# A two-layer decoder trunk on one core: order of VectorE's work around low halves, and where the modulation tiles stand

## The reference, cut to what matters

```python
cond = silu(c)
for layer in range(2):
    mod = cond @ ada_w[layer] + ada_b[layer]            # 2048 x 12288, one row of cond
    sh1, sc1, g1, sh2, sc2, g2 = split(mod, 6)
    h = rms_norm(x) * (1 + sc1) + sh1
    y = even_mixer(h, ...) if layer == 0 else odd_mixer(h, ...)
    x = x + g1 * y
    h = rms_norm(x) * (1 + sc2) + sh2
    gate, up = split(h @ ffn_w_in[layer], 2)            # 2048 x 11264
    x = x + g2 * ((silu(gate) * up) @ ffn_w_out[layer])
return rms_norm(x, final_norm)

# even_mixer: one projection 2048 x 6144; 8 heads "A" (causal attention over the 256 tokens)
# and 4 heads "B", each with two softmax maps and a 256-wide value:
w = p[map 0] - lam * p[map 1]                            # the "map combination"
yb = rms_norm(w @ v, subln_w) * (1 - lambda_init)        # the "output scaling" of B
# odd_mixer: 32 query heads of 64 on 4 key/value heads, window 128, a sink logit per head
```

## Time and profile before

| | us |
|---|---|
| median of 3 runs (2286.57 to 2287.35) | 2286.96 |
| the profiled execution | 2287.97 |
| its span in the trace | 2286.2 |
| TensorE busy | 2168.9 |
| VectorE busy | 1622.3 |
| ScalarE busy | 967.0 |

### The profile page before, as it was taken

One profiled execution on the slowest core, in us unless ns is written; L12 is line 12 of the kernel. 1 busy time (PEld: TensorE's weight loads), 2 busy tenths in 40 slices (PEclk: granted clock), 3 DMA queues, 4 the chain that ended last, 5 costly groups with the idle time before them and its releaser, 6 DMA issues.

```text
span 2286.2 us, 26487 instructions
## 1 busy us (share of the span) xinstructions
PE 2168.9 (95%) x10092; PEld 1802.7 (79%) x10092; DVE 1622.3 (71%) x1683; ACT 967.0 (42%) x1261; POOL 9.9 (0%) x22
## 2 busy tenths in 40 slices
PE   3789999989999999999998999989999999999997
PEld 2668878778888888888886888878888888888885
DVE  5989888887679988777678665577665554555454
ACT  4344444444443444434444444454443344434443
POOL 0000000000000000000000000000000000000000
PEclk9899999999999999999999999999999999999998
DMA  9968878667768999977675733347765555555533
GB/s 391 421 277 314 338 300 332 269 262 295 284 270 353 386 379 378 374 295 289 264 279 203 267 125 112 121 169 286 287 254 185 200 185 185 193 192 191 196 147 147
DMA packets 82448, 594.10 MB, mean 260 GB/s; under 512 B 9296, under 2 KB 9328, under 8 KB 10672
## 3 DMA queue, kind: packets, MB, share of 16 engines
q1 hardware_dynamic: 81072, 588.29, 66.9%
q0 software_dynamic: 1280, 4.51, 0.7%
HBM read 590.66 MB, written 2.10 MB: 259 GB/s over the span
## 4 chain that ended last, share of the span: by engine, by line
PE 48%; issue 36%; DVE 9%; ACT 3%; DMA 3%; DVEq 1%; SPq 0%; POOL 0%; ACTq 0%; POOLq 0%
PE ps L1240 15%; PE ps L1242 15%; PE ps L1241 15%; DVE w_lo L748 3%; DMA gate<-in_ada 2%; PE ps L1228 2%; DVE ada_raw L752 2%; ACT w_hi L452 1%; ACT gate L522 1%; ACT ada_raw L522 1%; DVE gate L752 0%; PE ps L1302 0%; PE ps L1297 0%; PE ps L1300 0%; DMA raw<-in_ab_in 0%
## 5 line engine op out<-in xcount | busy, mean ns | idle before, releaser
L748 DVE TENSOR_TENSOR w_lo<-raw,w_hi 128x1024 fp32r<-128x1024 f32 x728 | 881.2, 1223 | 508.5 <-ACT w_hi L452 503.4
L452 ACT ACTIVATE w_hi<-raw 128x1024 fp32r<-128x1024 f32 x728 | 763.5, 1060 | 1004.5 <-PE ps L1242 825.4
L1240 PE MATMUL ps<-w_hi,xT_hi 128*128 128x512 f32 x1952 | 775.8, 397 | 36.9 <-DVE xT_lo L952 26.5
L1242 PE MATMUL ps<-w_hi,xT_lo 128*128 128x512 f32 x1952 | 766.4, 393 | 0.0
L1241 PE MATMUL ps<-w_lo,xT_hi 128*128 128x512 f32 x1952 | 766.0, 392 | 0.0
L1240 PEld LDWEIGHTS ps<-w_hi,xT_hi 128*128 128x128 f32 x1952 | 369.9, 189 | 116.2 <-DVE xT_lo L952 28.8
L1242 PEld LDWEIGHTS ps<-w_hi,xT_lo 128*128 128x128 f32 x1952 | 370.3, 190 | 79.2
L1241 PEld LDWEIGHTS ps<-w_lo,xT_hi 128*128 128x128 f32 x1952 | 371.0, 190 | 75.0
L752 DVE SCALAR_TENSOR_TENSOR ada_raw<-ada_raw,cond 128x2048 f32<-128x2048 f32 x176 | 401.7, 2283 | 17.5 <-DMA ada_raw<-in_ada 16.5
L1240 PE MATMUL ps<-w_hi,hT_hi 128*128 128x512 f32 x960 | 376.3, 392 | 0.0
L1242 PE MATMUL ps<-w_hi,hT_lo 128*128 128x512 f32 x960 | 373.9, 389 | 0.0
(11 more groups left out here) (163 smaller groups left out, 834.6 us busy)
## 6 DMA issues: line engine op xcount, KB each, us to landing
ada_raw<-in_ada SPq DMA_DIRECT2D x176, 1024.0 KB, 6.4
raw<-in_ffn_in SPq DMA_DIRECT2D x176, 1024.0 KB, 4.8
raw<-in_ffn_out SPq DMA_DIRECT2D x88, 1024.0 KB, 4.9
raw<-in_ab_in SPq DMA_DIRECT2D x48, 1024.0 KB, 8.8
raw<-in_swa_in SPq DMA_DIRECT2D x20, 1024.0 KB, 6.1
raw<-in_ab_out SPq DMA_DIRECT2D x16, 1024.0 KB, 8.4
raw<-in_swa_out SPq DMA_DIRECT2D x16, 1024.0 KB, 4.8
spare<-in_ada SPq DMA_DIRECT2D x8, 1024.0 KB, 8.3
```

Of the source, the lines that this page charges most:

```text
L452: nc.scalar.activation(w_hi[:, p % PAIRS, :, :], raw[:, t % RAW, 2 * (p % 2):2 * (p % 2) + 2, :], ACT.Copy).then_inc(hi_ready, 1)
L748: tt(w_lo[:, p % PAIRS, :, :], raw[:, (p // 2) % RAW, 2 * (p % 2):2 * (p % 2) + 2, :], w_hi[:, p % PAIRS, :, :].bitcast(F32), ALU.subtract ...
L1240: mm(out, hi[:, kt, tok], w_hi[:, q % PAIRS, k, :], start=(kt == 2 * ps0), stop=False)
L1242: last = mm(out, lo[:, kt, tok], w_hi[:, q % PAIRS, k, :], start=False, stop=(kt == 2 * ps1 - 1))
```

## The change

Five edits, all in the order of work. No arithmetic is added or removed.

1. The tile count of a phase is now in units of 2 tiles instead of 4, and a phase can have a `lag`: no tiles behind its first `lag` pairs. `AB_IN` is split into `AB1` (one unit, 10 tiles, lag 4) and `AB23` (two units, 12 tiles each); `AB_OUT` has 14 tiles (12 before) with lag 7. In the first feed-forward the three runs have, per iteration, 6, 8, 4 tiles in the inner part (4, 8, 4 before) and 8, 4, 2 in the outer (8, 4, 4 before). `C_KV` has none (4 before). The second feed-forward is as it was.
2. In the key/value block the low halves 4 to 7 stand ahead of the clearing of `work`.
3. For B units the map combination stands ahead of the fifth low half, and in `ab` the tile of pair 5 stands ahead of it.
4. For B units in `ab` the output scaling stands ahead of the tile of pair 11.
5. In the odd layer the output scaling stands one pair earlier (9 instead of 10 in `C_DVE`) and is no longer a special case at the evacuations.

```diff
-    def __init__(self, prev, n, blocks, pairs, ada, src=None, src0=0, evacs=None):
+    def __init__(self, prev, n, blocks, pairs, ada, src=None, src0=0, evacs=None, lag=0):
...
     def ada_steps(self, p):
-        n = 4 * self.ada
-        return range(n * p // (2 * self.quads), n * (p + 1) // (2 * self.quads))
+        n = 2 * self.ada
+        if p < self.lag:
+            return range(0)
+        p, of = p - self.lag, 2 * self.quads - self.lag
+        return range(n * p // of, n * (p + 1) // of)
...
-TAIL_DVE = {3: "v", 4: "tops", 5: "recip", 8: "copy1", 10: "y", 13: "lo"}
+TAIL_DVE = {4: "tops", 8: "copy1", 13: "lo"}
...
-C_DVE = {4: "tops", 6: "recip", 7: "copy1", 8: "copy3", 10: "y", 11: "lo"}
+C_DVE = {4: "tops", 6: "recip", 7: "copy1", 8: "copy3", 9: "y", 11: "lo"}
...
-    AB_IN = phase(3, 3, 8, 3, src="ab_in", src0=12, evacs=2)
-    AB_OUT = phase(1, 4, 8, 3, src="ab_out")
+    AB1 = phase(1, 3, 8, 5, src="ab_in", src0=12, evacs=2, lag=4)
+    AB23 = phase(2, 3, 8, 6, src="ab_in", src0=24, evacs=2)
+    UNIT = [(AB0, 0), (AB1, 0), (AB23, 0), (AB23, 1)]
+    AB_OUT = phase(1, 4, 8, 7, src="ab_out", lag=7)
...
-            in_ada = (1, 2, 1)[s] if layer == 0 else int(s == 0)
-            out_ada = (2, 1, 1)[s] if layer == 0 else 0
+            in_ada = (3, 4, 2)[s] if layer == 0 else 2 * (s == 0)
+            out_ada = (4, 2, 1)[s] if layer == 0 else 0
...
-            C_KV = phase(1, 1, 8, 1, src="swa_in")
+            C_KV = phase(1, 1, 8, 0, src="swa_in")
...
             def ab(i, prev):
...
-                    ada_behind(AB_IN, i - 1, n)
+                    if prev == "A":
+                        ada_behind(*UNIT[i], n)
+                        continue
+                    if n == 4:
+                        ada_behind(*UNIT[i], 5)
+                        combine(i - 1)
+                    if n == 12:
+                        y_out(i - 1, prev)
+                    if n not in (5, 11):
+                        ada_behind(*UNIT[i], n)
+                    if n == 12:
+                        ada_behind(*UNIT[i], 11)
...
                 ab_stage(TAIL_DVE.get(n), 3, "B")
+                if n == 4:
+                    combine(3)
+                if n == 10:
+                    y_out(3, "B")
...
+            for p in range(AHEAD, 8):
+                lo(C_KV, 0, p)
             nc.vector.memset(work[:, 0:2048], 0.0)
-            for p in range(8):
-                if p >= AHEAD:
-                    lo(C_KV, 0, p)
-                ada_behind(C_KV, 0, p)
```

45 lines of the change are left out of this document (21 added, 24 removed).

## The result

| | before | after |
|---|---|---|
| median, us | 2286.77 (2286.23 to 2287.35, 4 runs) | 2265.46 (2263.70 to 2266.93, 4 runs) |
| profiled execution, us | 2287.97 | 2264.14 |
| its span, us | 2286.2 | 2262.3 |

The ratio is 0.9908, 95% interval 0.9896 to 0.9920. The change is faster by 21.3 us; forecast were 23.6 (2263.4).

The account below looks back on a forecast made before the run. TensorE, busy 95% of the span, was taken to set the end. Terms 4.0 + 3.3 + 5.9 - 1.5 + 7.3 + 4.6 = 23.6 us off 2287.97 gave 2264.4, less 1.01 for the median: 2263.4 us, range 2257.5 to 2273.

Parts of the forecast that it names:

- AB1: No tiles behind the first 4 pairs: TensorE's low-half waits of 1.40 and 2.57 us go, gain 4.0 us.
- Unit 2: Combination ahead of the fifth low half, scaling earlier: waits for transposes and scaling shrink or go, gain 3.3 us.
- Unit 3: Tail: waits of 2.23 and 1.90 us go, output products lose 1.77 us of low clock, gain 5.9 us.
- Key/value block: Low half 4 earlier, quads issued together: 4.93 us wait and 2.35 us of slow pair go, gain 7.3 us.
- Odd layer: Output scaling one pair earlier: TensorE's five waits for it, 4.7 us, nearly all go, gain 4.6 us.
- AB_OUT with the norm: 14 tiles in 25 pairs just fit on VectorE; TensorE waits 0.9, norm chain 0.6 late: cost 1.5 us.
- it fits by 4%: AB_OUT's transfers need 406 GB/s against 421 seen in the trace; late tiles were left to the range.
- rival A: AB_OUT eats more: each of 13 tiles 0.6 us late, 8 us on TensorE, 2271 us; chance 0.17.
- The sign of being wrong: TensorE's idle in AB_OUT and the norm grows by over 5 us, or low half 4 still waits.
- Rival B: Clock terms (1.8 + 2.35 us) absent and half the odd layer's 4.6 lost: 2270 us; chance 0.11.
- rival C: Slower than before: late tiles in AB_OUT stall TensorE, 7.3 us each; 2298 us with five; chance 0.04.
- Rival D: Waits move but TensorE's stay, ended by something beside VectorE: within 4 us of 2287; chance 0.06.

Follow-up runs that it names:

- experiment 9: Changed kernel with the B units' map combination and output scaling back in their old places, tiles as changed: 2268.15 us (one run).
- the pure wait: Changed kernel with four drained clearings of `work` ahead of low half 4 in the key/value block, no tiles there: 2275.06 us (one run).
- thin transfers: Changed kernel with AB_OUT's 14 tiles transferred in their first 128 of 2048 columns only, VectorE's work the same: 2262.42 us (one run).
- experiments 1: Changed kernel with the key/value block as before: four tiles again, clearing and first two tiles ahead of low half 4: median 2272.13 us, ratio to before 0.9935.
- 10: Changed kernel with the odd layer's output scaling again one pair later, ahead of the bias evacuation: 2270.21 us (one run).

## Why the prediction was right, and where it was not

The time (2263.4, measured 2265.5), the direction and the places were right; the cost in AB_OUT was not. Point by point:

- **AB1** (4.0, measured 4.5): both waits went but for 0.21 us, as the two rows said. `copy1`, whose wait went from 1.50 to 1.14 us, gives 0.4 more, and the rest is the overlap between products that each wait costs beside itself. No run undid this part; it rests on the rows of before and after.
- **Unit 2** (3.3, measured 4.8): undoing the order gives 3.1 back (experiment 9). From start to start the pairs with the two waits give 2.46 and 1.84 us, so the 0.4 us of waiting that I had left for the fifth low half did not come. Another 0.86 is a wait of 0.72 us for ScalarE ahead of the scores, in the trace of before and not in that of after, and 0.3 is lost near 357. This stretch scatters by itself, by up to 1.9 us.
- **Unit 3** (5.9, measured 6.3): the tiles leave, both waits go and the output products run at full rate; all three terms held. What I credited to the combination's new place was hardly needed: 0.3 us.
- **Key/value block** (7.3, measured 7.4): shown twice, by the undoing (6.6) and by the pure wait (its pair took 5.16 us at a clock of 0.50). The clearing's part, with the tiles gone, is 0.4. Whether tiles or SP's order would have cost it alone was not tried.
- **Odd layer** (4.6, measured 4.4): the four waits of 0.87 us give 1.08 each from start to start, as each also costs 0.2 us of overlap between products: 4.3. The fifth (1.26) gives nothing. Before, the evacuation of L1151 hid behind TensorE's wait for the scaling; now TensorE waits 1.14 us for it, and that pair takes 5.58 us as before. I had written that TensorE wants it three pairs later. In the last unit no scores stand between, and TensorE wants it at once.
- **AB_OUT with the norm** (-1.5, measured -5.1): the failed term. The queue was added up rightly. With thin transfers the stretch costs 1.3 us and VectorE is busy 59.81 of 61, and the one wait at the update has the size forecast. What failed is the step "it fits by 4%" for the transfers, with "a tile that lands late blocks the low halves behind it on VectorE. I let this in through the range": late landings were put at nothing in the sum. In their place the runs showed seven waits of ScalarE for late quads (24.8 us). VectorE had no slack to swallow its own 1.69 us of waiting for a high half, so the gate copy was late, for which I had named no wait (1.60). The size is that of rival A in small (3.6 us over the forecast instead of 8). Its reason was only in part right: a mean rate of 350 GB/s went with late quads and 404 did no harm, and VectorE waited for a tile only once (1.56 us). What came late are the quads, which SP issues together with a tile that has itself waited for VectorE.

The signs named beforehand say the same. The key/value block, the transposes, the output products and the odd layer's waits look as written. In AB_OUT VectorE is busy 56.39 of 61 us, 92% instead of over 95, and the transfers run at 350 GB/s instead of near 400. The sign of being wrong, over 5 us more of idle TensorE there and in the norm, was nearly met: the two stretches took 5.1 us longer, of which the profile counts 3.9 as idle (9.3 us against 5.4) and the rest as busy TensorE, as the overlap lost at a wait is.

The total was closer than its parts, and that was luck. Of the 3.6 us missed in AB_OUT, 2.4 were made up by AB1, unit 2 and unit 3, which came out larger for reasons of their own; 0.9 more went in the other parts, and 23.6 - 3.6 + 2.4 - 0.9 = 21.5. Rival B falls (both clock terms were there, and the odd layer kept its gain), rival C as well: the late quads never gave a stall like that of the key/value block. Rival D falls in experiments 1, 9 and 10, each of which gives its part back when undone; the part of AB1 and the missing tiles of unit 3, some 10 us together, were never put back, and for them the waits gone from the rows have to do.

## What to carry to other kernels

When work is moved into a stretch, add up the queue of the engine that does it, and then also the transfers it brings: in one issue order a filler transfer can delay the needed one behind it, and an engine without slack passes that on. Put filler where the trace shows that engine idle (ahead of the step that waits, with its transfer issued earlier); spread evenly over the pairs, the same count cost 2.7 us more here. And price the work behind a long wait at the low clock: here that was 1.7 to 2.4 us more for the next pair behind waits of 2.89 us and over.
